# A hybrid mixer and product-key layer: x and the rows of w_in by partition quarters, x turned by VectorE

## The reference, cut to what matters

```python
D_MODEL, SEQ, CHUNK = 2048, 256, 64          # float32, one layer
def reference(x, ...):
    h = x
    proj = einsum('bsd,dn->bsn', h, w_in)     # 2048 channels -> 7184 columns
    gq, gk, gv, gr, glr, rq, rk, rv, rr = split(proj)
    log_a = log_sigmoid(glr @ w_gate_up + b_gate) / 16
    o_gla = head_norm(gla_chunk_causal(gq, gk, gv, log_a)) * silu(gr)
    o_ret = head_norm(retention_chunk_causal(rotary(rq), rotary(rk), rv)) * silu(rr)
    h = layer_norm(ALPHA * h + concat(o_gla, o_ret) @ w_out)
    q = h @ w_q; scores = q . subkeys; top 16 x 16 -> top 16 of 128*128 experts, 8 heads
    ffn = sum over experts of gate * gelu(peer_u[e] . h) * peer_v[e]
    return layer_norm(ALPHA * h + ffn)
```

## Time and profile before

| what | us |
|---|---|
| median of three runs | 1930.41 |
| the profiled execution, its own time | 1929.52 |
| its span, first to last instruction | 1927.6 |
| TensorE busy | 1905.5 (99%) |
| GpSimd (POOL) busy | 1441.9 (75%) |
| VectorE busy | 1338.1 (69%) |
| ScalarE busy | 988.5 (51%) |
| TensorE's share of the chain that ended last | 85% |

### The profile page before, as it was taken

One profiled execution on the slowest core, in us unless ns is written; L12 is line 12 of the kernel. 1 busy time (PEld: TensorE's weight loads), 2 busy tenths in 40 slices (PEclk: granted clock), 3 DMA queues, 4 the chain that ended last, 5 costly groups with the idle time before them and its releaser, 6 DMA issues.

```text
span 1927.6 us, 34659 instructions
## 1 busy us (share of the span) xinstructions
PE 1905.5 (99%) x10830; PEld 1667.1 (86%) x10830; DVE 1338.1 (69%) x2305; ACT 988.5 (51%) x1518; POOL 1441.9 (75%) x964
## 2 busy tenths in 40 slices
PE   9999999999999999999999999999999999999997
PEld 9999888888998888888888888888888888888886
DVE  1755012213688877765789999998788888888888
ACT  4544334435445556557445445545555555555554
POOL 6887878887878898989778787876476677567541
PEclk9999999999999999999999999999999999999999
DMA  8555647567869887778877777777899999999993
GB/s 294 171 154 163 206 149 225 180 225 188 213 146 204 189 187 184 174 179 194 246 173 178 173 174 168 177 166 198 312 328 334 341 326 338 340 366 356 368 322 134
DMA packets 197498, 440.60 MB, mean 229 GB/s; under 512 B 29409, under 2 KB 40545, under 8 KB 196273
## 3 DMA queue, kind: packets, MB, share of 16 engines
q1 hardware_dynamic: 181712, 384.40, 69.7%
q0 software_dynamic: 14416, 50.61, 7.6%
q10 hardware_dynamic: 1296, 4.65, 0.7%
HBM read 426.79 MB, written 12.78 MB: 228 GB/s over the span
## 4 chain that ended last, share of the span: by engine, by line
PE 85%; POOL 4%; DMA 4%; issue 3%; DVE 2%; ACT 1%; DVEq 0%; SPq 0%; ACTq 0%; POOLq 0%
PE ps L1822 26%; PE ps L1777 22%; PE ps L1778 11%; PE ps L1517 7%; PE ps L1519 7%; PE ps L1518 7%; POOL w_lo L1391 3%; PE ps L1759 3%; DMA v_raw<-in_peer_v 3%; POOL u_lo L1429 1%; DMA u_raw<-in_peer_u 1%; PE ps L1633 1%; DVE u_t L1055 0%; PE ps L1742 0%; DVE v_lo L1284 0%
## 5 line engine op out<-in xcount | busy, mean ns | idle before, releaser
L1429 POOL TENSOR_TENSOR u_lo<-u_t,u_hi 128x512 fp32r<-128x512 f32 x512 | 653.8, 1300 | 128.5 <-ACT u_hi L637 125.5
L1777 PE MATMUL ps<-xT,u_hi 128*128 128x512 f32 x2048 | 724.9, 398 | 0.9 <-POOL u_lo L1429 0.9
L1778 PE MATMUL ps<-xT,u_lo 128*128 128x256 f32 x2048 | 572.7, 280 | 0.0
L1391 POOL TENSOR_TENSOR w_lo<-raw,w_hi 128x1024 fp32r<-128x1024 f32 x174 | 431.2, 2492 | 100.8 <-ACT w_hi L506 94.4
L637 ACT ACTIVATE u_hi<-u_t 128x512 fp32r<-128x512 f32 x512 | 321.2, 632 | 351.2 <-DVE u_t L1055 351.0
L1777 PEld LDWEIGHTS ps<-xT,u_hi 128*128 128x128 f32 x2048 | 384.3, 188 | 89.3 <-POOL u_lo L1429 1.3
L1055 DVE STREAM_TRANSPOSE u_t<-u_raw 128x512 f32<-128x512 f32 x512 | 354.2, 700 | 96.9 <-PE ps L1778 54.8
L1778 PEld LDWEIGHTS ps<-xT,u_lo 128*128 128x128 f32 x2048 | 386.6, 189 | 0.0
L506 ACT ACTIVATE w_hi<-raw 128x1024 fp32r<-128x1024 f32 x175 | 184.8, 1059 | 273.3 <-PE ps L1519 261.5
L1454 POOL DMA_INDIRECT sp_rows<-in_peer_v,sp_at x128 | 182.6, 1426 | 151.2 <-DVE far_sum L1268 131.7
L1822 PE MATMUL ps<-v_lo,m_hi 128*128 128x512 f32 x882 | 270.3, 375 | 0.0
(11 more groups left out here) (235 smaller groups left out, 2693.6 us busy)
## 6 DMA issues: line engine op xcount, KB each, us to landing
u_raw<-in_peer_u SPq DMA_DIRECT2D x512, 256.0 KB, 4.8
v_raw<-in_peer_v SPq DMA_DIRECT2D x252, 512.0 KB, 6.2
raw<-in_w_in SPq DMA_DIRECT2D x111, 512.0 KB, 3.8
raw<-in_w_out SPq DMA_DIRECT2D x32, 512.0 KB, 3.8
raw<-in_w_peer_q SPq DMA_DIRECT2D x128, 128.0 KB, 4.7
act_dram<-act_w ACTq DMA_DIRECT2D x4, 1024.0 KB, 6.8
act_dram<-far_act SPq DMA_DIRECT2D x62, 64.0 KB, 5.0
x_again<-in_x SPq DMA_DIRECT2D x1, 2048.0 KB, 8.0
```

Source lines behind the costliest of these rows:

```text
L1391: pool.tensor_tensor(w_lo[:, k, :], raw[:, k, :], w_hi[:, k % HI_RING, :].bitcast(F32), ALU.subtract).then_inc(lo_done, 1)
L1429: pool.tensor_tensor(u_lo[:, r, :], u_t[:, r, :], u_hi[:, r, :].bitcast(F32), ALU.subtract).then_inc(ulo_done, 1)
L1777: pe.matmul(acc, u_hi[:, r, c], xT[:, :, kt, :], start=kt == 0, stop=False)
L1778: ins = pe.matmul(acc[:, 0:T], u_lo[:, r, c], xT_hi[:, kt, :], start=False, stop=kt == KT - 1)
```

## The change

x is loaded in two tiles. Channels 0 to 511 go as before to `x_first`, with tokens on partitions, and TensorE turns them (turns 0 and 1). The other 1536 go to `x_perm`, in which partition 32 q + l holds tokens l, 32 + l, ... and the q-th quarter of the 1536 channels. VectorE's 32 by 32 transpose turns 64 of its columns over eight token blocks (128 x 512 elements) into the two channel blocks of one step, `x_t`, from which ScalarE takes the high and VectorE the low part. The channels then lie in another order, so the rows of w_in for steps 2 to 7 are loaded in that order, four DMAs of 32 partitions a step, in all 14 groups, and the last twelve blocks of `glr_raw` too. Two of x's parts are issued by POOL (`load_x(pool, 0, 4, ...)`, four DMAs with pieces of 512 B), ahead of its first w_lo; the other by SP behind step 4 (pieces of 1 KB). TensorE's turns 2 to 7 are gone. At the start of the V stage the loads of V tiles 2 and 3 are issued half by half, as the quarters of the last two U tiles that they overwrite are read.

```diff
+        x_first = at("x_first", WRK + 13 * K, [P, TT, COL])
+        x_perm = at("x_perm", WRK + 17 * K, [P, T // 32, D - COL >> 2])
+        x_t = at("x_t", HT + 16 * K, [P, KT, T])
...
+        win_rows = win[COL:D, :].rearrange("(q f l) n -> q l f n", q=4, f=KT - 4)
+        x_rows = x[0].rearrange("(b l) d -> l b d", l=32)[:, :, COL:D].rearrange("l b (q d) -> q l b d", q=4)
...
+        def load_x(eng, f0, n, done):
+            d = slice(32 * f0, 32 * (f0 + n))
+            for q in range(4):
+                eng.dma_start(x_perm[32 * q:32 * q + 32, :, d], x_rows[q][:, :, d]).then_inc(done, 16)
 
         @block.sync
             def load_step(g, k, w, col):
                 sp.wait_ge(step_free, STEPS * g + k + 1)
+                if w is win and k >= 2:
+                    for q in range(4):
+                        sp.dma_start(raw[32 * q:32 * q + 32, k, :].rearrange("p (k n) -> p k n", k=2),
+                                     win_rows[q][:, 2 * k - 4:2 * k - 2, bass.ds(col, COL)]).then_inc(raw_in[k], 16)
+                    return
...
-            for b in range(1, 4):
-                load_step(0, 2 * b, win, GQ)
-                sp.dma_start(*x_cols(b * COL, COL)).then_inc(x_in[b], 16)
-                load_step(0, 2 * b + 1, win, GQ)
-            sp.dma_start(glr_raw[:], win[:, GLR:GLR + P].rearrange("(k p) n -> p k n", p=P)).then_inc(glrw_in, 16)
+            load_step(0, 2, win, GQ)
+            load_step(0, 3, win, GQ)
+            load_step(0, 4, win, GQ)
+            load_x(sp, 4, 8, x_in[2])
+            for k in range(5, STEPS):
+                load_step(0, k, win, GQ)
+            sp.dma_start(glr_raw[:, 0:4], win[0:COL, GLR:GLR + P].rearrange("(k p) n -> p k n", p=P)).then_inc(glrw_in, 16)
+            for q in range(4):
+                sp.dma_start(glr_raw[32 * q:32 * q + 32, 4:KT], win_rows[q][:, :, GLR:GLR + P]).then_inc(glrw_in, 16)
...
-            for s in range(2):
-                sp.wait_ge(ut_done, 4 * (P - 1) + 4 * s)
-                load_v(s, s)
-                far_store(P // 2 - 4 + s, s)
-            sp.wait_ge(uparts_free, UR + 4 * P)
-            for s in range(2, 4):
-                load_v(s, s)
+            def quarters_read(left):
+                sp.wait_ge(uparts_free, UR + 4 * P - left)
+
+            sp.wait_ge(ut_done, 4 * (P - 1))
+            load_v(0, 0)
+            far_store(P // 2 - 4, 0)
+            sp.wait_ge(ut_done, 4 * P)
+            load_v(1, 1)
+            quarters_read(4)
+            load_v(2, 2, halves=(1,))
+            far_store(P // 2 - 3, 1)
+            quarters_read(2)
+            load_v(3, 3, halves=(0,))
+            quarters_read(0)
+            load_v(2, 2, halves=(0,))
+            load_v(3, 3, halves=(1,))
...
         def act_turn(act, use, c):
+            if use == 0 and c >= 2:
+                act.wait_ge(x_turned, c - 1)
+                act.activation(xT_hi[:, 2 * c:2 * c + 2, :], x_t[:, 2 * c:2 * c + 2, :], ACT.Copy).then_inc(tr_hi, 1)
+                return
...
-            for c in range(1, 8):
-                turn_lo(dve, 0, c)
+            def x_turn(c):
+                dve.wait_ge(x_in[1 if c < 4 else 2], 64)
+                dve.transpose(x_t[:, 2 * c:2 * c + 2, :].rearrange("p f (b l) -> p b f l", l=32),
+                              x_perm[:, :, 64 * (c - 2):64 * (c - 1)].rearrange("p b (f l) -> p b f l", l=32)).then_inc(x_turned, 1)
+
+            turn_lo(dve, 0, 1)
+            x_turn(2)
+            for c in range(2, 8):
+                if c < 7:
+                    x_turn(c + 1)
+                dve.wait_ge(tr_hi, c + 1)
+                pair = slice(2 * c, 2 * c + 2)
+                dve.tensor_tensor(xT_lo[:, pair, :], x_t[:, pair, :], xT_hi[:, pair, :].bitcast(F32), ALU.subtract).then_inc(tr_lo, 1)
...
+            pool.wait_ge(x_half, 16)
+            load_x(pool, 0, 4, x_in[1])
             for k in range(2):
                 pool.wait_ge(hi_done, k + 1)
...
-            ready = lambda c: (x_in[c // 2] if c else x_half, 16)
-            turn(x_sb, 0, 0, *ready(0))
+            turn(x_first, 0, 0, x_half, 16)
             for k in range(STEPS):
                 pe.wait_ge(tr_lo, k + 1)
-                if k < 2:
-                    steps_n(0, (k,), between=lambda: turn(x_sb, 0, k + 1, *ready(k + 1)))
-                else:
-                    steps_n(0, (k,))
-                if 0 < k < 6:
-                    turn(x_sb, 0, k + 2, *ready(k + 2))
+                steps_n(0, (k,), between=(lambda: turn(x_first, 0, 1, x_in[0], 16)) if k == 0 else None)
```

More of the change, by code:

```diff
@@ L125, in build @@
         mixc = at("mixc", WRK, [P, sum(MIX.values())])
-        x_sb = at("x_sb", WRK + 13 * K, [P, TT, D])
+        x_first = at("x_first", WRK + 13 * K, [P, TT, COL])
+        x_perm = at("x_perm", WRK + 17 * K, [P, T // 32, D - COL >> 2])
+        x_t = at("x_t", HT + 16 * K, [P, KT, T])
         o_sb = at("o_sb", WRK + 13 * K, [P, TT, D])
@@ L262, in build @@
         step_free, hi_done, lo_done, acc_free = sem("step_free"), sem("hi_done"), sem("lo_done"), sem("acc_free")
+        x_turned = sem("x_turned")
         tr_done, tr_hi, tr_lo = sem("tr_done"), sem("tr_hi"), sem("tr_lo")
@@ L301, in build, with raw_count @@
         v_rows = peer_v[0].rearrange("(i j) d -> i j d", j=P)
-        def raw_count(g):
-            return 16 * (g + 1) if not isinstance(g, int) or g < O_END else 16 * O_END + 64 * (g + 1 - O_END)
+        def raw_count(g, k):
+            of_in, of_out, of_q = min(g + 1, B_END), min(max(g + 1 - B_END, 0), O_END - B_END), max(g + 1 - O_END, 0)
+            return (16 if k < 2 else 64) * of_in + 16 * of_out + 64 * of_q
         def used(g, k=STEPS - 1):
@@ L327, in _ @@
             sp.sem_inc(step_free, RING)
-            x_cols = lambda c0, n: (x_sb[:, :, c0:c0 + n], x[0].rearrange("(a p) d -> p a d", p=P)[:, :, c0:c0 + n])
+            x_cols = lambda c0, n: (x_first[:, :, c0:c0 + n], x[0].rearrange("(a p) d -> p a d", p=P)[:, :, c0:c0 + n])
             sp.dma_start(*x_cols(0, COL // 2)).then_inc(x_half, 16)
@@ L425, in _, with load_v @@
             sp.sem_inc(v_free, VRING)
-            def load_v(i, s, freed=None):
-                for h in range(2):
+            def load_v(i, s, freed=None, halves=range(2)):
+                for h in halves:
                     if freed is not None:
@@ L482, in _, with turned @@
             sp.wait_ge(out_done, 16 * TT * 4)
+        def turned(use, c):
+            return (0, 2, 10)[use] + c + 1
         def act_turn(act, use, c):
-            act.wait_ge(tr_done, use * 8 + c + 1)
+            if use == 0 and c >= 2:
+                act.wait_ge(x_turned, c - 1)
+                act.activation(xT_hi[:, 2 * c:2 * c + 2, :], x_t[:, 2 * c:2 * c + 2, :], ACT.Copy).then_inc(tr_hi, 1)
+                return
+            act.wait_ge(tr_done, turned(use, c))
             act.activation(xT_hi[:, 2 * c:2 * c + 2, :].rearrange("p a b -> p (a b)"), bank(4 + c % 4), ACT.Copy).then_inc(tr_hi, 1)
         def act_scaled_turn(act, c):
-            act.wait_ge(tr_done, 16 + c + 1)
+            act.wait_ge(tr_done, turned(2, c))
             for k in range(2):
@@ L503, in hi_steps @@
                 for k in ks:
-                    act.wait_ge(raw_in[k], raw_count(g))
+                    act.wait_ge(raw_in[k], raw_count(g, k))
                     act.wait_ge(step_free, used(g, k - HI_RING))
@@ L554, in _ @@
             later_turns(0, 0, lead=3)
-            act.wait_ge(glrw_in, 16)
+            act.wait_ge(glrw_in, 80)
             act.activation(glr_both[:], glr_raw[:], ACT.Copy).then_inc(glrw_hi, 1)
```

## The result

| | before | after |
|---|---|---|
| median of 22 runs each, same chip (us) | 1929.26 (1924.09 to 1935.47) | 1932.57 (1928.90 to 1935.76) |
| ratio after to before, 95% interval | | 1.002 [1.0014, 1.0027] |
| profiled execution: its time, span | 1929.52, 1927.6 | 1932.58, 1930.4 |

By the ratio the changed kernel is slower by 0.2%, 3.9 us (2.7 to 5.2); the two medians differ by 3.3. The forecast was +0.8 us, at 1931.2, and the time lies within the range.

A forecast was written before the change was run, and what follows sets the result against it. TensorE, busy 1905.5 of 1927.6 us, was taken as the bound. Group 0 at +2.3 and V at -1.5 gave +0.8 on the profiled 1929.52, so 1930.3, plus 0.9 to the median: 1931.2 us, range 1926.5 to 1935.6.

The forecast's parts named there:

- The rate and the landing: Group 0 loads: quartered transfers run at 240 GB/s, x_in[2] lands at 22.3 us, step 3 starts at 23.8.
- The reason given for it: Group 0 loads: partition quarters, not piece size, cause 240 instead of 390 GB/s; a 32-partition block reaches eight of 16 ports.
- Rival A: Group 0 loads: quarters from two queues cost no speed, x_in[2] there by 17.6, time 1926.1 us; chance 0.13.
- The steady state: Groups 1 to 13: 26 loads a group instead of eight stay hidden from TensorE; cost 0, bounds 0 and +2 us.
- Step 4 starts at 27.0: Group 0: raw 5 at 24.5, then 1.06 + 0.60 on ScalarE and 0.69 on VectorE; group ends at 38.4, +2.3 us.
- rival B: Group 0: clock falls in the wait before step 3 and short pieces lengthen that wait; 1935.9 us, chance 0.20.
- Waits of steps 0 to 2, POOL's loads: Start of group 0: POOL's four loads, 3.8 to 8.1 us, delay w_lo(0); cost nothing, covered by the wait for x.
- The V start: Start of V: earlier half loads of tiles 2 and 3 remove TensorE's 1.51 us wait for tile 4; -1.5 us.
- rival C: Start of V: far_store comes late and its 0.8 us replaces the 1.5 gained; 1933.5 us, chance 0.12.
- The sum: Whole kernel: +2.3 in group 0 and -1.5 at V give +0.8 us; median forecast 1931.2 us.

The follow-up runs named there:

- experiment 1: A kernel of loads alone, the layer left out: 383 GB/s over 128 partitions, 234 in partition quarters, 301 with quarters from two queues.
- experiment 4: Changed kernel with w_in loaded over 128 partitions in natural channel order, x still in quarters; 1940.78 us, ratio 1.0007 to the kernel before.
- experiment 7: Changed kernel with VectorE's turned x in PSUM instead of SBUF; 1932.94 us, one run.
- experiment 3: Changed kernel with the old order of loads at the start of V; 1948.34 us, ratio 1.0055 to the kernel before.
- experiment 9: Changed kernel with 3 and 7 idle TensorE matmuls in the waits before steps 2 and 3, turned x in SBUF; 1934.13 us, one run.
- experiment 10: Changed kernel with turned x in PSUM and 3 and 7 idle TensorE matmuls before steps 2 and 3; 1931.26 us, one run.
- experiments 2 and 12: Kernel before with only the new order of loads at the start of V, on two chips; ratios 0.9989 and 0.9986.
- 11: Changed kernel with x_in[2] issued ahead of raw 4, turned x in PSUM, idle matmuls before steps 2, 3 and 4; 1933.50 us, ratio 1.003 to the kernel before.
- 5: Changed kernel with x_turn(4) behind VectorE's subtraction for c = 3; 1933.26 us, one run.

## Why the prediction came out as it did

**The rate and the landing: right.** 240 GB/s were forecast for 10 to 22 us and 240 measured; x_in[2] at 22.3 against 22.07, step 3 at 23.8 against 23.41, raw 5 at 24.5 against 24.01. The rate of another stage's quarters carried over. The reason given for it was half right: experiment 1 shows the same rate for quarters by themselves, experiment 4 that w_in's quarters are not needed for it. Putting w_in back in the old form moved the gate matmuls by 0.6 us and x's landing by 0.2; by the prediction's own argument, with 1.57 MB at 240 and 1.57 MB at 390 GB/s, x would have landed 2.5 us sooner. Rival A (quarters from two queues cost nothing) is out: two queues gave 301 at best by themselves and 240 in the kernel. The steady state, priced at nothing, was right too: from the gate matmuls to the first U matmul the two profiles differ by 0.2 us, and the gate weights landed at 34.0, where 33.8 was forecast.

**"Step 4 starts at 27.0": the step that failed.** It started at 28.13, 1.1 us later, and from there four steps end at 39.5; the gate matmuls came at 39.76 instead of 38.4. Two things delayed it, and the sum had neither.
- The subtraction was priced at 0.69 from the earlier trace rows, a row with its operand in PSUM. With both operands in SBUF beside POOL's w_lo it took 2.45. POOL's instruction begins at 25.15 and lasts 2.38, VectorE's begins at 25.62 and ends at 28.07, 0.54 behind POOL's end: it waited for POOL. The Trainium skill (SBUF — State Buffer, "Who interferes with whom") states it: a VectorE instruction with two SBUF inputs and a GpSimd one that reads SBUF exclude each other, and the later one waits for the whole of the first. The trace agrees: 0.65 with POOL idle (22.70), 2.45 and 2.27 with POOL in front, 0.69 again in experiment 7. By that sentence the term could have been estimated beforehand from the prediction's own numbers: with raw 5 at 24.5, POOL's low part of step 5 runs from 25.6 to 27.9, and the subtraction, ready at 26.2, would end at about 28.5 instead of 26.9.
- The clock fell after the 3.23 us wait, from 24.6 to about 28. Step 3 took 4.5 us instead of 2.84. That is rival B, in part (the 1.2 GHz level, seen by spacing and by the granted clock): the fall came, but 1.2 us after TensorE had started again and for about 3 us, not at once and for 6.2.

In the changed kernel the clock let step 3 end at 27.9 and the subtraction ended at 28.07, so either alone puts step 4 near 28. Three traces with the same edit of x bear this out: both together here, the subtraction alone in experiment 3, the clock alone in experiment 4. Taking away one gave nothing (experiments 7 and 9), and with both gone raw 5 itself came too late (experiment 10, 39.6; 1.6 us later than here). By these numbers 38.4 would need all three; no run has them together.

**Waits of steps 0 to 2, POOL's loads: right in effect.** POOL's four loads took 0.65 us each, below the 0.94 to 2.02 of the bounds. They delay w_lo(0) by half a microsecond, and the wait for x covers it. Step 2 also waits 1.53 us for x_in[1], which landed at 14.9; that too was covered: the 4.7 us of waiting that were forecast before step 3 came as 1.53 before step 2 and 3.23 before step 3.

**The V start: right.** -1.5 was forecast. The wait at tile 4 is gone in ten of the eleven traces with the new V start (0.84 us remain in experiment 9; 1.51 and 1.09 with the old one), and far_store isn't late, so rival C is out. The stage is 2.8 us shorter in the profiled pair, and the kernel 2.1 and 2.7 us faster in experiments 2 and 12, with intervals that reach from 5.2 gained to 0.6 lost. What exceeds 1.5 us isn't explained: with the new start V lasts from 571 to 577 us in the nine traces that weren't taken on the chip of experiments 1 to 4, and its other waits for m_lo come and go between them (none to six), so that their fall from 3.8 to 1.3 us can't be put down to the edit.

**The sum.** The kernel before starts the gate matmuls at 36.1, 34.9 and 35.6 in the three profiles with its group 0, the changed one at 39.8 and 39.7: a cost of 4.2 us, where +2.3 was forecast from the one profile at 36.13. The scatter before the change is that of the clock's first rise: the spacing goes from 0.21 to 0.12 us at 13.4 in the first of these profiles, at about 10.5 in the second and 12.1 in the third. With -1.5 to -2.8 for V this makes +1.4 to +2.7; measured is +3.9 (2.7 to 5.2). The rest, if it is one, is below what the intervals can tell. That the time itself came within 1.4 us of the forecast is partly luck. In the profiled pair a loss of 3.6 for 2.3 and a gain of 2.8 for 1.5 cancel to the forecast's +0.8, while over all runs the difference is +3.9; and the forecast started from a median of three runs, 1930.41, that lay 1.2 above the one of 22. Why experiment 3 lost 10.7 us on its chip stays open.

## What to carry to other kernels

Before a load is cut to fit a cheap transpose, price every load in the same stretch at the rate of the cut one, and look for such a rate elsewhere in the trace. When an operand moves from PSUM to SBUF, look at what POOL does at that moment and on whose path the instruction lies. Where a wait is followed by a slow clock, count both, and don't expect anything from removing one of several causes that are due at the same time.

## What the runs showed that I had not expected

- Loads into 32 partitions at a time run at 234 GB/s and into 128 at 383, both with all DMA engines' time taken; from two queues 301. Beside x's quartered short pieces the 128-partition loads lose their rate too (245 in all).
- The load whose source has a slowest dimension of 4 used a quarter of the engines: share 0.26, 102 GB/s.
- Of VectorE and POOL, whichever comes second waits. In the first steps it is POOL: its two half w_lo took 1305 and 1773 ns, the second with VectorE's w_lo half begun at the same moment (both from 9.0). The tile w_lo in the changed kernel, 4 to 36 us (duration ns min/median/max, first and last start):

```profile
L850 DVE TENSOR_TENSOR w_lo<-raw,w_hi x2: 691/692/692, 6.0 to 9.0; 128x512 fp32r<-128x512 f32 x2
L1458 POOL TENSOR_TENSOR w_lo<-raw,w_hi x2: 1305/1539/1773, 7.6 to 9.0; 128x512 fp32r<-128x512 f32 x2
```

- The clock fell to 0.50 in or behind waits of 3.2 to 4.0 us (after, 3, 4, 7, 11) and of 1.76, 2.24 and 1.72 us (9, and twice in 5). It held at 1.00 behind waits of 0.94 and 0.52 (10), but also of 1.53 (after) and 2.13 us (before step 2 in 3). So the length of the one wait doesn't decide it. The moment differs between runs of the same transfers too: in the changed kernel 1.2 us after work had begun again, in 3 and 7 within the wait.
